# The last recurrent head: two halves of a gate product, and splits and a fetch that come later

## The chip, the cores and the metric

The kernel runs on one core of a Trainium2 chip. The metric is the device time of one execution in microseconds (us), the median of several runs. TensorE is called PE here, VectorE DVE, ScalarE ACT, GpSimd POOL and SyncE SP, as in the profile.

## What is computed

Two transformer blocks over 1024 tokens of width 1024, in float32. The change lies in the first block, in its HGRN2 mixer (six heads of 128 channels, chunks of 64 tokens) and at the start of the output product that follows it:

```python
h = rms_norm(x, norm_mix_g)
u_pool, q_raw, f_raw, i_raw, g_raw = split(h @ w_in)
log_f = log(lb + (1 - lb) * sigmoid(f_raw)); k = (1 - lb) * sigmoid(-f_raw)
q = silu(q_raw); v = i_raw
# per chunk: b = cumsum(log_f)
scores = einsum(q, k, exp(b_t - b_s))          # causal
o = scores @ v + (q * exp(b)) @ state
state = exp(b_last) * state + (k * exp(b_last - b)).T @ v
o = rms(o) * norm_g * silu(g_raw)
x = x + concat([y_pool, y_hgrn]) @ w_out
```

Here the lower bound lb is zero (one layer), so the decay of a step is sigmoid(f_raw).

## The kernel before

Every product of the model is made three times, high part by high part, low by high and high by low, in matmuls of 128x512. Features lie on the 128 partitions and tokens along the free dimension. A product of one weight tile (128 output features, 1024 inputs) takes eight contraction tiles k; each k takes 6 matmuls (three terms, two halves of 512 tokens).

**The program is written out by hand, engine by engine**, with semaphores: each engine works through its own list in order. For a head of the recurrence, `product` (line 798 is its matmul) makes the four projections f, q, i (the value) and g (the output gate). DVE takes each of them out of PSUM (`take`, line 2056). The causal scores are built in seven levels, from neighbouring tokens up to half chunks. For level l, ACT copies two halves of `kd_t` and `qd_t` into a buffer `e_t` (lines 1526 and 1527), PE multiplies them (`level`, line 925), DVE merges the result into `s_t` (`merge`, line 2170; the diagonal at 2155) and multiplies both tiles by decays to prepare the next level (`move`, three instructions, lines 2145 to 2147). ACT's copy for level l waits for move l-1 and for PE's level l-2. Then PE transposes `zv` and `kd_t` (`turn`, line 837), and the state updates, the outputs and the mean of their squares follow (lines 975, 984 and 986, 992).

**Fillers.** `head(h, meanwhile)` on PE has eight places at which another product is put. The first five heads run in a loop and put the next head's projections there. The last head (its code stands behind the loop, in ACT's and DVE's lists under `last`) has its own gate product at place 0, whole, and then parts of the output product of the block: `begin_out(t, part)` makes the contraction tiles `part` of output tile t. An output tile needs the mixed tiles `mix1`, split into `h_hi` (ACT, line 1509, `mix1_hi`) and `h_lo` (DVE, line 2128, `mix_lo`). `h_hi` and `h_lo` hold the input of the projections until then, so ACT waits in front of the first `mix1_hi` until the gate product is finished (`tile_done`, T_OUT1).

**Weights.** POOL splits every weight tile in two instructions (a cast, line 713, and a subtraction, line 715) in the order of use. The split of output tile 1 waits for the end of the gate product, since it overwrites that product's weights. The split of tile 2 comes behind it in POOL's list, and that of tile 3 behind that; tile 3's waits also for the transpose of `zv` and for `sg_t`, over which it is laid. SP loads a raw tile when the split of the tile two places earlier is done.

**The residual** `x_t` shares its memory with `mix1`. It was stored in DRAM (`x_spill`) and is fetched again by one DMA from ACT's queue (line 1562), once seven mixed tiles are split. DVE needs it at line 2301, when the first output tile is finished.

Of the kernel before, what the change touches and what calls it, by code (L numbers as in the profile page):

```python
# [25 lines left out]
ACT = mybir.ActivationFunctionType  # L26
# [5 lines left out]
KT = D // P  # L32
# [8 lines left out]
HEADS = 6  # L41
# [63 lines left out]
T_HEADS = T_POOL + POOL_W // P  # L105
# [60 lines left out]
def two_blocks(nc, dram, out):  # L166
    ctx = ExitStack()
    with ctx:
# [3 lines left out]
        def at(name, shape, address, dtype=F32):  # L172
            return nc.alloc_sbuf_tensor_at(name, shape, dtype, offset=address)
# [4 lines left out]
        h_hi = at("h_hi", [P, KT, SEQ], A_HI, F32R)  # L178
        h_lo = at("h_lo", [P, KT, SEQ], A_LO, F32R)
# [138 lines left out]
        def banks(b, n=2):  # L318
            return psum[:, b:b + n, :].rearrange("p b t -> p (b t)")
# [76 lines left out]
        zf_ready, zq_ready, zv_ready, zg_ready = (sem(f"z{n}_ready") for n in "fqvg")  # L396
# [4 lines left out]
        g_gate = sem("g_gate")  # L401
# [7 lines left out]
        v_turned = sem("v_turned")  # L409
        v_ready = sem("v_ready")  # L410
# [10 lines left out]
        y_ready = sem("y_ready")  # L421
# [362 lines left out]
        def _(pe):  # L784
            def product(n, slot, first_bank, hi, lo, part=range(KT), split=None, halves=range(2), weights=None):

                w_tile_hi, w_tile_lo = weights or (w_hi[:, slot, :], w_lo[:, slot, :])

                pe.wait_ge(weight_split, n + 1)
                for k in part:
                    if split is not None:
                        pe.wait_ge(*split(k))
                    wh, wl = w_tile_hi[:, k * P:(k + 1) * P], w_tile_lo[:, k * P:(k + 1) * P]
                    for j, (w, a) in enumerate(((wh, hi), (wh, lo), (wl, hi))):
                        for t in halves:
                            last = pe.matmul(psum[:, first_bank + t, :], w, a[:, k, t * HALF:(t + 1) * HALF],  # L798
                                             start=(k == 0 and j == 0), stop=(k == KT - 1 and j == 2))
                if part[-1] == KT - 1 and halves[-1] == 1:  # L800
                    last.then_inc(tile_done, 1)
                return last
# [98 lines left out]
                pe.wait_ge(zf_ready, h + 1)  # L901
                product(h * 4 + (T_HEADS + 2), 0, 0, h_hi, h_lo, part)

            def project_g(h):

                pe.wait_ge(zq_ready, h + 1)
                product(h * 4 + (T_HEADS + 3), 1, 2, h_hi, h_lo)

            first_half, second_half = range(KT // 2), range(KT // 2, KT)

# [113 lines left out]
            for j in range(2):  # L1024
                pe.wait_ge(pool_p_ready, j + 1)
                for t in range(2):
                    last = pe.matmul(psum[:, 4 + 2 * j + t, :], pool_w[:, j, :],
                                     pool_p[:, j, t * HALF:(t + 1) * HALF], start=True, stop=True)
# [10 lines left out]
            def begin_out(t, part):  # L1039

                pe.wait_ge(*((zv_ready, HEADS), (zg_ready, HEADS), (o_log, HEADS + 1))[t])
                out_tile(t, part)

            def begin_rest():
                begin_out(1, range(5, 7))
                begin_out(2, range(7))

            head(HEADS - 1, [lambda: project_g(HEADS - 1), lambda: begin_out(0, range(0, 4)),
                             lambda: begin_out(0, range(4, 7)), lambda: begin_out(1, [0]), lambda: begin_out(1, [1]),
                             lambda: begin_out(1, [2, 3]), lambda: begin_out(1, [4]), begin_rest])  # L1050
            for t in range(3):
                out_tile(t, [KT - 1])

# [372 lines left out]
        def _(act):  # L1426
# [87 lines left out]
            def head(h, last):  # L1514
                def level(l):


                    if l == 0:
                        act.wait_ge(qd_start, h + 1)
                    else:  # L1520
                        act.wait_ge(level_moved, h * LEVELS + l)
                    if l >= 2:

                        act.wait_ge(level_done, h * (LEVELS + 1) + l)
                    e = level_parts(e_t[:, l % 2, :], l)
                    act.activation(e[:, :, 0, :], level_parts(kd_t[:, :], l)[:, :, 0, :], ACT.Copy)
                    act.activation(e[:, :, 1, :], level_parts(qd_t[:, :], l)[:, :, 1, :], ACT.Copy)\
                       .then_inc(level_ready, 1)

                def begin_mix(*tiles):  # L1530
                    if last:
                        for d in tiles:
                            mix1_hi(d)


                act.wait_ge(zq_ready, h + 1)
                act.activation(q_t[:, :], zq[:, :], ACT.Sigmoid).then_inc(q_gate, 1)
                act.wait_ge(zf_ready, h + 1)
                act.activation(decays[:, 0:SEQ], zf[:, :], ACT.Sigmoid).then_inc(f_ready, 1)
                act.activation(kd_t[:, :], zf[:, :], ACT.Sigmoid, scale=-1.0).then_inc(kd_start, 1)  # L1540
                act.activation(k_t[:, :], zf[:, :], ACT.Sigmoid, scale=-1.0).then_inc(k_ready, 1)
                act.wait_ge(kd_start, h + 1)
                level(0)
                level(1)

                act.wait_ge(y_ready, h + 1)
                act.wait_ge(zg_ready, h + 1)
                act.activation(sg_t[:, :], zg[:, :], ACT.Sigmoid).then_inc(g_gate, 1)
                if last:

                    act.wait_ge(tile_done, T_OUT1)
                begin_mix(0, 1)
                level(2)
                begin_mix(2, 3, 4, 5, 6)
                level(3)

                act.wait_ge(v_turned, h + 1)
                act.activation(v_tok[:, :, :].rearrange("p c v -> p (c v)"), banks(6), ACT.Copy).then_inc(v_ready, 1)
                if last:

                    act.wait_ge(mix_split, KT - 1)
                    act.dma_start(x_t[:, 0:KT - 1, :].rearrange("p d t -> p (d t)"),
                                  x_spill[:, 0:(KT - 1) * SEQ]).then_inc(x_back, 16)
                level(4)
                level(5)
                level(6)

                act.wait_ge(kd_turned, h + 1)
                act.activation(kd_tok[:, :, :].rearrange("p c k -> p (c k)"), banks(6), ACT.Copy)\
                   .then_inc(kd_tok_ready, 1)  # L1570

                act.wait_ge(o_done, h + 1)
                act.activation(e_t[:, 1, :], banks(6), ACT.Square).then_inc(o_sq, 1)
                act.wait_ge(o_mean, h + 1)
                act.activation(e_t[:, 0, :], banks(4), ACT.Ln, scale=1.0 / P, bias=eps1[:, :]).then_inc(o_log, 1)
                act.wait_ge(o_log, h + 2)
                act.activation(e_t[:, 0, :], e_t[:, 0, :], ACT.Exp, scale=-0.5).then_inc(o_inv, 1)
# [423 lines left out]
        def _(dve):  # L2001
# [56 lines left out]
            def take_f(h):  # L2058
                take(zf, h * 4 + T_HEADS, 6 if isinstance(h, int) and h == 0 else 0, zf_ready)
# [7 lines left out]
            def take_g(h):  # L2067
                take(zg, h * 4 + (T_HEADS + 3), 2, zg_ready)
# [62 lines left out]
            def head(h, last):  # L2131
# [5 lines left out]
                def move(l):  # L2137


                    n, s = SEQ >> (l + 1), 1 << l  # L2140
                    decay, twice = decay_of(l), 2 * SEQ - (2 * SEQ >> (l + 1))
                    q, k = level_parts(qd_t[:, :], l)[:, :, 1, :], level_parts(kd_t[:, :], l)[:, :, 0, :]

                    dve.wait_ge(level_ready, h * LEVELS + (l + 1))
                    dve.tensor_tensor(q, q, decay[:, :, 0:1].to_broadcast([P, n, s]), ALU.mult)
                    dve.tensor_tensor(k, k, decay[:, :, 1:2].to_broadcast([P, n, s]), ALU.mult)
                    dve.tensor_tensor(decays[:, twice:twice + n], decay[:, :, 0], decay[:, :, 1], ALU.mult)\
                       .then_inc(level_moved, 1)
# [24 lines left out]
                def begin_mix(*tiles):  # L2173
                    if last:
                        for d in tiles:
                            mix_lo(0, d, mix1)
# [6 lines left out]
                dve.tensor_tensor(qd_t[:, :], q_t[:, :], decays[:, 0:SEQ], ALU.mult).then_inc(qd_start, 1)  # L2183
                move(0)
                move(1)
                take_g(h)
                merge_diagonal()
                merge(0, 4)
                begin_mix(0)
                move(2)  # L2190
                begin_mix(1)
                merge(1, 5)
                begin_mix(2, 3)

                dve.wait_ge(g_gate, h + 1)
                dve.tensor_tensor(sg_t[:, :], zg[:, :], sg_t[:, :], ALU.mult).then_inc(sg_ready, 1)
                move(3)
                begin_mix(4, 5, 6)
                if not last:

                    dve.wait_ge(k_ready, h + 1)
                    take_f(h + 1)
                merge(2, 4)
                move(4)
                merge(3, 5)
                move(5)
                merge(4, 6)
# [597 lines left out]
```

## Time and profile before

| | us |
|---|---|
| median of 3 runs | 2596.09 (2593.04 to 2596.7) |
| the profiled execution | 2595.25 |
| its span, first to last instruction | 2593.5 |
| PE busy | 2545.7 (98% of the span) |
| DVE busy | 1514.2 (58%) |
| POOL busy | 947.8 (37%) |
| ACT busy | 676.4 (26%) |

The last head runs from about 381 us to 439 us of the span, under 3% of it. A busy time over the whole kernel says little about such a short stretch. There the timelines of the single engines are to be read side by side: where PE is idle and who released it, and what the releasing engine did before.

### The profile page before, as it was taken

The page shows a single profiled execution, that of the slowest core. Times are in us where ns is not written, and L with a number is a line of the kernel's source. Part 1 is how long each engine was busy: PE and PEld are TensorE (multiplying, and loading weights), DVE is VectorE, ACT ScalarE, POOL GpSimd, SP SyncE. Part 2 cuts the span into 40 slices and gives each one's busy share as a digit, 9 for nine tenths or more (in the row PEclk, how much of TensorE's full clock was granted, in tenths as well). Part 3 has the DMA queues.
Part 4 walks back from the last instruction along what each step waited for, and adds up shares of the span by engine and source line. Part 5 has one row for each costly group of instructions (what it writes and reads, how often), then busy time and mean ns, then how long its engine had stood idle before and what let it go on. Part 6 is the DMA issues. An engine that isn't in the chain of part 4 may idle for free.

```text
span 2593.5 us, 37645 instructions
## 1 busy us (share of the span) xinstructions
PE 2545.7 (98%) x14373; PEld 2081.0 (80%) x14373; DVE 1514.2 (58%) x1617; ACT 676.4 (26%) x921; POOL 947.8 (37%) x558
## 2 busy tenths in 40 slices
PE   8999998999999999999999999999999999999997
PEld 7788886878888888887777788888888888888886
DVE  6755566843335666667777786354455555555555
ACT  4233443443332000013333313201211111111114
POOL 2222222387874333333222232333333333333334
PEclk9999998999999999999999999999999999999999
DMA  6111112333434222223111111113111111111111
GB/s 208 39 41 32 32 40 90 124 98 121 129 108 170 97 97 97 97 73 123 33 39 38 39 41 49 49 49 114 45 45 48 49 49 49 49 49 49 49 49 74
DMA packets 212830, 186.04 MB, mean 72 GB/s; under 512 B 15343, under 2 KB 184986, under 8 KB 211738
## 3 DMA queue, kind: packets, MB, share of 16 engines
q1 hardware_dynamic: 189604, 122.92, 15.6%
q10 hardware_dynamic: 23158, 62.18, 6.6%
q8 instruction: 46, 0.75, 0.1%
q14 instruction: 22, 0.18, 0.0%
HBM read 151.51 MB, written 35.33 MB: 72 GB/s over the span
## 4 chain that ended last, share of the span: by engine, by line
PE 86%; DVE 9%; ACT 2%; issue 2%; DMA 1%; DVEq 0%; ACTq 0%; SPq 0%
PE psum L798 48%; PE psum L817 16%; PE psum L1089 11%; PE psum L1299 3%; PE psum L837 1%; PE psum L925 1%; DVE ffn_gate L2693 1%; DVE x_t L2326 1%; PE psum L1228 1%; DVE h_lo L2025 1%; PE psum L1413 1%; PE psum L1209 1%; DVE sq_sum L2020 1%; DVE ffn_val L2697 0%; DVE ffn_gate L2697 0%
## 5 line engine op out<-in xcount | busy, mean ns | idle before, releaser
L713 POOL CAST w_hi<-w_raw 128x1024 fp32r<-128x1024 f32 x180 | 204.8, 1138 | 1489.4 <-issue 763.9
L798 PE MATMUL psum<-h_hi,w_hi 128*128 128x512 f32 x1744 | 551.8, 397 | 9.1 <-DVE h_lo L2128 6.5
L798 PE MATMUL psum<-h_lo,w_hi 128*128 128x512 f32 x1744 | 539.6, 391 | 0.0
L798 PE MATMUL psum<-h_hi,w_lo 128*128 128x512 f32 x1744 | 538.9, 390 | 0.0
L715 POOL TENSOR_TENSOR w_lo<-w_raw,w_hi 128x1024 fp32r<-128x1024 f32 x180 | 478.2, 2657 | 14.4
L798 PEld LDWEIGHTS psum<-h_hi,w_hi 128*128 128x128 f32 x1744 | 322.1, 188 | 83.6 <-issue 18.9
L798 PEld LDWEIGHTS psum<-h_hi,w_lo 128*128 128x128 f32 x1744 | 328.2, 188 | 69.6
L798 PEld LDWEIGHTS psum<-h_lo,w_hi 128*128 128x128 f32 x1744 | 328.1, 188 | 69.5
L2326 DVE TENSOR_TENSOR x_t<-x_t,psum 128x512 f32<-128x512 f32 x416 | 281.1, 684 | 171.2 <-PE psum L817 162.9
L2685 DVE TENSOR_TENSOR ffn_z<-psum,rinv 128x1024 f32<-128x1024 f32 x44 | 53.9, 1225 | 273.9 <-PE psum L798 266.0
L817 PE MATMUL psum<-down_hi,w_hi 128*128 128x512 f32 x512 | 199.6, 390 | 2.2 <-DVE x_t L2326 2.0
L817 PE MATMUL psum<-down_hi,w_lo 128*128 128x512 f32 x512 | 199.2, 389 | 0.0
L817 PE MATMUL psum<-down_lo,w_hi 128*128 128x512 f32 x512 | 199.2, 389 | 0.0
L2497 DVE SCALAR_TENSOR_TENSOR conv_t<-u_t,cols,conv_t 128x1024 f32<-128x1024 f32 x120 | 179.6, 1496 | 2.4
L817 PE MATMUL psum<-ffn_hi,w_hi 128*128 128x512 f32 x320 | 127.0, 397 | 4.0 <-DVE x_t L2326 3.4
L817 PE MATMUL psum<-ffn_lo,w_hi 128*128 128x512 f32 x320 | 124.7, 390 | 0.0
L817 PE MATMUL psum<-ffn_hi,w_lo 128*128 128x512 f32 x320 | 124.7, 390 | 0.0
L817 PEld LDWEIGHTS psum<-down_hi,w_hi 128*128 128x128 f32 x512 | 96.1, 188 | 23.7 <-DVE x_t L2326 3.9
L817 PEld LDWEIGHTS psum<-down_hi,w_lo 128*128 128x128 f32 x512 | 96.1, 188 | 20.1
L817 PEld LDWEIGHTS psum<-down_lo,w_hi 128*128 128x128 f32 x512 | 96.1, 188 | 19.6
L1745 ACT ACTIVATE down_hi<-down_in 128x1024 fp32r<-128x1024 f32 x32 | 32.1, 1052 | 280.3 <-DMA down_in<-act_rows 280.3
L753 POOL TENSOR_TENSOR mlp_s_lo<-mlp_s_sum,mlp_s_hi 128x512 fp32r<-128x512 f32 x60 | 78.1, 1335 | 19.9 <-ACT mlp_s_hi L1633 19.9
(374 smaller groups left out, 3910.5 us busy)
## 6 DMA issues: line engine op xcount, KB each, us to landing
w_raw<-in_w_in SPq DMA_DIRECT2D x124, 256.0 KB, 3.1
w_raw<-in_w_up SPq DMA_DIRECT2D x120, 256.0 KB, 3.2
w_raw<-in_w_down SPq DMA_DIRECT2D x108, 256.0 KB, 2.7
act_rows<-mlp_a ACTq DMA_DIRECT2D x32, 512.0 KB, 3.6
down_in<-act_rows ACTq DMA_DIRECT2D x32, 512.0 KB, 3.6
w_raw<-in_w_out SPq DMA_DIRECT2D x32, 256.0 KB, 3.1
mlp_raw<-in_w_up SPq DMA_DIRECT2D x32, 256.0 KB, 3.7
x_in<-in_x SPq DMA_DIRECT2D x8, 512.0 KB, 8.1
```

Of the source, the lines that this page charges most:

```text
L713: pool.tensor_copy(hi, w_raw[:, slot, :]).then_inc(weight_hi, 1)
L715: pool.tensor_tensor(lo, w_raw[:, slot, :], hi.bitcast(F32), ALU.subtract).then_inc(weight_split, 1)
L753: done = pool.tensor_tensor(lo[:, :], full[c], hi[:, :].bitcast(F32), ALU.subtract)
L798: last = pe.matmul(psum[:, first_bank + t, :], w, a[:, k, t * HALF:(t + 1) * HALF], start=(k == 0 and j == 0), stop=(k == KT - 1 and j == 2))
L817: last = pe.matmul(psum[:, 4 + g % 4, :], w, a[k][:, t * HALF:(t + 1) * HALF], start=(k == 0 and j == 0), stop=(k == 1 and j == 2))
L837: last = pe.transpose(psum[:, dst_bank + c // 4, (c % 4) * P:(c % 4 + 1) * P], block_in, ident[:, :])
L1089: last = pe.matmul(psum[:, bank, :], w, a[:, :], start=start and kk == part[0] and j == 0, stop=stop and kk == part[-1] and j == 2, skip_g ...
L1299: last = pe.matmul(psum[:, bank + t, :], w, a[:, t * HALF:(t + 1) * HALF], start=(k == 0 and j == 0), stop=(k == 3 and j == 2))
L1745: act.activation(down_hi[b][j][:, :], down_in[b][j][:, :], ACT.Copy).then_inc(act_hi_ready, 1)
L2326: dve.tensor_tensor(x_d, x_d, psum[:, 4 + g % 4, :], ALU.add).then_inc(down_added, 1)
L2497: dve.scalar_tensor_tensor(acc, u_t[:, c % 2, tap:tap + SEQ], w, acc, ALU.mult, ALU.add)\
L2685: dve.tensor_tensor(ffn_z[:, part, :], banks(2 * part), rinv[:, :], ALU.mult).then_inc(ffn_read, 1)
```

## The change

On PE the last head's gate product is cut in two. Its first four contraction tiles stay in place 0, and the other four go to place 1, behind levels 0 and 1. The parts of the output product move one place back and are grouped otherwise. On ACT the order of the last head becomes levels 0 to 3, the value's copy, the gate's sigmoid, the high parts of mixed tiles 0 to 3, level 4, the high parts of 4 to 6, level 5, the fetch of the residual, level 6. On DVE the gate is taken behind merge 1 instead of behind move 1, and the low parts follow the gate's multiplication. In the loop's five heads nothing changes but the place of one conditional that does not apply to them.

```diff
-            def project_g(h):
+            def project_g(h, part=range(KT)):
                 pe.wait_ge(zq_ready, h + 1)
-                product(h * 4 + (T_HEADS + 3), 1, 2, h_hi, h_lo)
+                product(h * 4 + (T_HEADS + 3), 1, 2, h_hi, h_lo, part)
...
-            head(HEADS - 1, [lambda: project_g(HEADS - 1), lambda: begin_out(0, range(0, 4)),
-                             lambda: begin_out(0, range(4, 7)), lambda: begin_out(1, [0]), lambda: begin_out(1, [1]),
-                             lambda: begin_out(1, [2, 3]), lambda: begin_out(1, [4]), begin_rest])
+            head(HEADS - 1, [lambda: project_g(HEADS - 1, first_half), lambda: project_g(HEADS - 1, second_half),
+                             lambda: begin_out(0, range(0, 4)), lambda: begin_out(0, range(4, 7)),
+                             lambda: begin_out(1, [0]), lambda: begin_out(1, [1, 2]), lambda: begin_out(1, [3, 4]),
+                             begin_rest])
...
                 level(0)
                 level(1)
-
-                act.wait_ge(y_ready, h + 1)
-                act.wait_ge(zg_ready, h + 1)
-                act.activation(sg_t[:, :], zg[:, :], ACT.Sigmoid).then_inc(g_gate, 1)
+                if not last:
+                    gate()
+                level(2)
+                level(3)
+                take_v()
                 if last:
-
+                    gate()
                     act.wait_ge(tile_done, T_OUT1)
-                begin_mix(0, 1)
-                level(2)
-                begin_mix(2, 3, 4, 5, 6)
-                level(3)
-
-                act.wait_ge(v_turned, h + 1)
-                act.activation(v_tok[:, :, :].rearrange("p c v -> p (c v)"), banks(6), ACT.Copy).then_inc(v_ready, 1)
+                begin_mix(0, 1, 2, 3)
+                level(4)
+                begin_mix(4, 5, 6)
+                level(5)
                 if last:
 
                     act.wait_ge(mix_split, KT - 1)
                     act.dma_start(x_t[:, 0:KT - 1, :].rearrange("p d t -> p (d t)"),
                                   x_spill[:, 0:(KT - 1) * SEQ]).then_inc(x_back, 16)
-                level(4)
-                level(5)
                 level(6)
...
                 move(0)
                 move(1)
-                take_g(h)
+                if not last:
+                    take_g(h)
                 merge_diagonal()
                 merge(0, 4)
-                begin_mix(0)
                 move(2)
-                begin_mix(1)
                 merge(1, 5)
-                begin_mix(2, 3)
+                if last:
+                    take_g(h)
+                    move(3)
 
                 dve.wait_ge(g_gate, h + 1)
                 dve.tensor_tensor(sg_t[:, :], zg[:, :], sg_t[:, :], ALU.mult).then_inc(sg_ready, 1)
-                move(3)
-                begin_mix(4, 5, 6)
+                begin_mix(0, 1)
                 if not last:
+                    move(3)
 
                     dve.wait_ge(k_ready, h + 1)
                     take_f(h + 1)
+                begin_mix(2)
                 merge(2, 4)
+                begin_mix(3)
                 move(4)
+                begin_mix(4, 5, 6)
                 merge(3, 5)
```

`gate` and `take_v` are the two pieces of ACT's list that were written in line before.

## Rows read from the trace of the kernel before

**Rows 1.** The page, part 4: shares of the chain that ended last.
```profile
PE 86%; DVE 9%; ACT 2%; issue 2%; DMA 1%; DVEq 0%; ACTq 0%; SPq 0%
```

**Rows 2.** Chain in order of time, 355 to 470 us: start, us, what.
```profile
439.31 27.24 PE psum L798 x120
```

**Rows 3.** PE's timeline, 345 to 470 us: start, us, instruction, count [idle before <-releaser].
```profile
391.71 0.76 PE L942 MATMUL psum<-q_t,k_t 128*32 128x32 f32 x64
395.70 0.31 PE L925 MATMUL psum<-e_t 128*32 128x16 f32 x12 [2.20 <-issue]
402.52 1.19 PE L798 MATMUL psum<-h_hi,w_hi 128*128 128x512 f32 x2 [6.51 <-DVE h_lo L2128]
...
408.11 0.83 PE L798 MATMUL psum<-h_hi,w_hi 128*128 128x512 f32 x2
411.09 1.04 PE L837 MATMUL psum<-ident,zv 128*128 128x128 f32 x8
...
425.78 1.09 PE L837 MATMUL psum<-ident,kd_t 128*128 128x128 f32 x8
```

**Rows 4.** DVE's timeline of the same stretch.
```profile
389.51 0.69 DVE L2145 TENSOR_TENSOR qd_t<-qd_t,decays 128x512 f32<-128x512 f32 x1 [1.34 <-ACT e_t L1527]
...
392.75 0.77 DVE L2145 TENSOR_TENSOR qd_t<-qd_t,decays 128x512 f32<-128x512 f32 x1 [1.34 <-ACT e_t L1527]
393.45 2.82 DVE L2146 TENSOR_TENSOR kd_t<-kd_t,decays 128x512 f32<-128x512 f32 x1
396.19 1.25 DVE L2147 TENSOR_TENSOR decays<-decays 128x256 f32<-128x256 f32 x1
397.37 1.21 DVE L2056 TENSOR_TENSOR zg<-psum,rinv 128x1024 f32<-128x1024 f32 x1
398.50 1.33 DVE L2155 COPY_PREDICATED s_t<-pair_mask,psum 128x1024 f32<-128x1024 uint32 x1
400.02 1.30 DVE L2170 COPY_PREDICATED s_t<-pair_mask,psum 128x512 f32<-128x512 uint32 x1 [0.18 <-DVE s_t L2155]
...
411.12 3.50 DVE L2128 TENSOR_TENSOR h_lo<-mix,h_hi 128x1024 fp32r<-128x1024 f32 x3
414.52 0.72 DVE L2170 COPY_PREDICATED s_t<-pair_mask,psum 128x512 f32<-128x512 uint32 x1
416.27 2.27 DVE L2145 TENSOR_TENSOR qd_t<-qd_t,decays 128x512 f32<-128x512 f32 x1 [1.03 <-ACT e_t L1527]
```

**Rows 5.** POOL's timeline, 330 to 500 us.
```profile
391.94 1.04 POOL L713 CAST w_hi<-w_raw 128x1024 fp32r<-128x1024 f32 x1 [7.35 <-issue]
393.06 2.66 POOL L715 TENSOR_TENSOR w_lo<-w_raw,w_hi 128x1024 fp32r<-128x1024 f32 x1
395.67 1.50 POOL L713 CAST w_out_hi<-w_raw 128x1024 fp32r<-128x1024 f32 x1
397.25 2.42 POOL L715 TENSOR_TENSOR w_out_lo<-w_raw,w_out_hi 128x1024 fp32r<-128x1024 f32 x1
412.29 3.22 POOL L713 CAST w_out_hi<-w_raw 128x1024 fp32r<-128x1024 f32 x1 [12.63 <-PE psum L837]
415.59 2.40 POOL L715 TENSOR_TENSOR w_out_lo<-w_raw,w_out_hi 128x1024 fp32r<-128x1024 f32 x1
```

**Rows 6.** ACT's timeline, 345 to 470 us.
```profile
387.20 1.05 ACT L1541 ACTIVATE k_t<-zf 128x1024 f32<-128x1024 f32 x1
...
392.02 0.70 ACT L1527 ACTIVATE e_t<-qd_t 128x512 f32<-128x512 f32 x1
398.68 1.06 ACT L1548 ACTIVATE sg_t<-zg 128x1024 f32<-128x1024 f32 x1 [5.96 <-DVE zg L2056]
```

**Rows 7.** Busy time by stretch; PEclk is the granted TensorE clock (1.00 is 2.4 GHz).
```profile
396.00:402.00 6.00, 0.01 (x1) 0.00 (x0) 5.82 (x6) 3.33 (x4) 3.58 (x2) 0.69 0.46 138
406.00:408.00 2.00, 2.00 (x6) 1.61 (x5) 2.00 (x3) 2.00 (x4) 0.00 (x0) 0.50 0.00 0
```

**Rows 8.** DMA issues by line, 355 to 480 us: queue, count, KB each, us to landing.
```profile
x_t<-x_spill ACTq DMA_DIRECT2D x1, 3584.0 KB, 12.6
```

More of the change, by code:

```diff
@@ L1542, in head, with gate, take_v @@
                 act.wait_ge(kd_start, h + 1)
+                def gate():
+                    act.wait_ge(y_ready, h + 1)
+                    act.wait_ge(zg_ready, h + 1)
+                    act.activation(sg_t[:, :], zg[:, :], ACT.Sigmoid).then_inc(g_gate, 1)
+                def take_v():
+                    act.wait_ge(v_turned, h + 1)
+                    act.activation(v_tok[:, :, :].rearrange("p c v -> p (c v)"), banks(6), ACT.Copy).then_inc(v_ready, 1)
                 level(0)
                 level(1)
-                act.wait_ge(y_ready, h + 1)
-                act.wait_ge(zg_ready, h + 1)
-                act.activation(sg_t[:, :], zg[:, :], ACT.Sigmoid).then_inc(g_gate, 1)
+                if not last:
[3 more added lines that the diff above has]
+                take_v()
                 if last:
+                    gate()
                     act.wait_ge(tile_done, T_OUT1)
-                begin_mix(0, 1)
-                level(2)
-                begin_mix(2, 3, 4, 5, 6)
-                level(3)
-                act.wait_ge(v_turned, h + 1)
-                act.activation(v_tok[:, :, :].rearrange("p c v -> p (c v)"), banks(6), ACT.Copy).then_inc(v_ready, 1)
+                begin_mix(0, 1, 2, 3)
+                level(4)
+                begin_mix(4, 5, 6)
+                level(5)
                 if last:
```

## The prediction

> **What bounds the kernel now.** I read the shares of the chain that ended last first: PE holds 86% of it and DVE 9% [rows 1]. Behind the last head PE runs without a gap, 120 matmuls in 27.24 us, or 0.227 us each, so six matmuls (one contraction tile k) cost 1.36 us [rows 2]. The time of the kernel therefore moves by as much as the point moves at which that last block starts: 439.31 us. Everything after it is the same program with the same distances.
>
> So the question is what sets 439.31. PE's timeline comes next. PE finishes the gate product at 391.71, makes the diagonal and levels 0 and 1, stops for 2.20 us in level 1 with no releaser shown, and then is idle for 6.51 us until DVE has split the first mixed tile [rows 3]. That idle time is what the change can fill. But PE is not what is late there. DVE's timeline shows a queue that hardly pauses from 392.75 until its last moves: its waits in the rows are fractions of a microsecond up to about 1 us, while single instructions take four times their usual time [rows 4]. POOL's timeline, laid beside it, shows why. The multiplication of `kd_t` at 393.45 takes 2.82 us where one of this shape takes 0.69, and it ends just after POOL's subtraction (393.06 to 395.72). The `decays` product at 396.19 waits out POOL's cast (395.67 to 397.17), and the one at 416.27 takes 2.27 us beside POOL's subtraction (415.59 to 417.99). Instructions that read PSUM, as the gate's take at 397.37 and the merge at 398.50, keep their 1.2 to 1.3 us beside POOL's subtraction of 397.25 to 399.67 [rows 4, 5]. **DVE instructions with both inputs in SBUF and POOL's splits exclude each other; those with an input in PSUM do not.** In this stretch DVE loses (2.82 - 0.69) + (1.25 - 0.4) + (2.27 - 0.69) = 4.6 us to it. The 0.4 is my estimate for 256 columns, between the 0.69 of 512 and a fixed part.
>
> **The change, part by part.**
>
> *The gate product in halves.* Its start on PE is 391.71 - 48 x 0.227 = 380.8 [rows 2, 3]; the first 24 matmuls end at 386.3. The diagonal needs `k_t`, which ACT ends at 388.25 [rows 6], and level 1 needs ACT's copy that ends at 392.72 [rows 6]. So PE now idles about 2 us ahead of the diagonal and again ahead of level 1, ends level 1 at about 393.4, and starts the second half there. At the full rate that half takes 5.45 us and ends at 398.9.
>
> The clock adds to that. In the kernel before the granted clock averages 0.69 over 396 to 402 and is 0.50 in 406 to 408 (1.2 GHz): it fell after PE had given up full-size matmuls at 391.7 and done only small ones and nothing [rows 3, 7]. The new order gives up full-size matmuls for 393.4 - 386.3 = 7.1 us, and before they were missing for 10.8 us. I take it that the clock falls here too, as this is the nearest row. The 12 matmuls from 402.52 to 408.11 then took 5.59 us instead of 2.72, so a fall costs 2.9 us [rows 3]; not falling costs 0. I take 2.9 and get **T = 401.7 for the end of the gate product** (398.9 if the clock stays).
>
> The 2.20 us stop in level 1 has no releaser and 180 small matmuls in front of it [rows 3]. It cost nothing before, since PE was waiting for DVE afterwards. In the new order it would lie before T. I take 0, since PE now idles twice ahead of that place and whatever is fetched has time to arrive, with 2.2 as the other end. The Trainium skill (Runtime: NRT & Kernel Launch, Instruction fetch mechanics) says that the instruction buffer is refilled in blocks while the engine runs and that crossing a block is mostly hidden; by it the term is 0 too, and the row before shows a stop that is not hidden, if it is that.
>
> *DVE until T.* Move 1 is no longer beside POOL's splits, because these wait for the gate product's end. It ends at 392.75 + 0.6 + 0.6 + 0.3 = 394.3 instead of 397.4. Diagonal and merge 0 (1.15 each), move 2 (0.6 + 0.6 + 0.2) and merge 1 (1.15) follow: 399.2. ACT makes the copies for levels 2 and 3 meanwhile. DVE then waits for T: **a new wait of 2.5 us**, and behind it are queued the take, moves 3 to 6, merges 2 to 6 and all seven splits.
>
> *DVE after T.* Durations from start to start are 0.1 less than in the rows. Take 1.13, move 3 1.3, gate multiplication 1.14, splits 0 to 2 3.4: 7.0 us in all. ACT does not hold it up: transpose (1.0, rows 3), value copy 1.0 and sigmoid 1.0 are done at T + 3.1, and one high part per 0.96 follows.
>
> POOL, however, starts the split of output tile 1 at T, that of tile 2 right behind and that of tile 3 behind that: three casts of 1.04 and three subtractions of 2.4, 10.3 us [rows 5]. Before, these lay at 391.9 to 399.7 and at 412.3 to 418, and 4.6 us of them hurt. Now all stand beside the take (1.1 us hidden) and the pile of SBUF instructions behind it. If the two take turns, as at 393.45 and 396.19, the seven DVE microseconds become 7.0 + 9.3 = 16.3: split 2 ends at T + 0.1 + 16.3 = 418.1. The rest has POOL out of its way: merge 2 0.65, split 3 1.14, move 4 1.3, splits 4 to 6 3.4, merge 3 0.65, move 5 1.27: 426.5. ACT's copy for level 6 takes 1.15 to 427.7, move 6 1.25 to 428.9. The transpose of `kd_t` on PE then ends at 428.9 + 0.15 + 0.9 = **429.9, against 426.9 before** (425.78 + 1.09, rows 3).
>
> The contention has a lower end. At 411.12 DVE made three splits in 3.50 us, one after the other, while POOL's cast, ready at 412.29, took 3.22 instead of 1.04 [rows 4, 5]: there POOL waited for a whole streak. If it does so again behind the gate's multiplication, part of its work moves beside merges and waits and some 2 us are saved. If there were no contention at all, 9.3 would be. I take turns, since two of the three collisions went that way, and keep 2 us below for the range.
>
> The Trainium skill (SBUF — State Buffer, SBUF: two separate sides) says that such a DVE instruction and a GpSimd one take a shared pair of ports whole, first come first served. It agrees with 2.82 us at 393.45, and speaks against this change. It says nothing of who is next when both wait, which is where the 2 us lie.
>
> *PE after the transpose.* Before, from 426.87 to 439.31, 12.44 us, with four k tiles as fillers. The new list has tile k 0 of output tile 1, then 1 and 2, then 3 and 4 there: five. The one more costs 1.36, as nothing else is late: 13.7 us, 429.9 + 13.7 = 443.6. All other fillers fit into the time in which PE waits for DVE: the mixed tiles arrive every 1.14 us or slower and cost 1.36.
>
> *The residual's fetch.* Its 3.5 MB take 12.6 us [rows 8]. The last split that it waits for ends at about 424.6, so it lands at 437.2, and the first addition comes over 14 us after 443.6: nothing. ACT's level 6 stands behind that wait in its queue, but needs move 5, which DVE makes after those splits anyway. Output tiles 2 and 3 are needed after 443.6, and POOL is done by about 418: nothing.
>
> **Sum.** 443.6 - 439.31 = +4.3 us. Split by cause: 2.5 for the wait for T, 9.3 - 4.6 = 4.7 for more contention, 1.4 for the k tile, and 4.3 less for DVE's old pauses, which the new waits swallow. On the profiled execution that is 2599.5; the median of the runs lies 0.84 above it, so 2600.4. As most bounds lie below, I say 2600.
>
> **Rivals.**
> 1. *The clock does not fall* in the seven microseconds. T is 398.9, the sum +4.3 - 2.8 = +1.5: 2597.6. For it: two of the gaps are short, with matmuls between. Against it: the fall in the rows after a like pause.
> 2. *POOL stays out of the way* (its instructions wait for DVE's streaks, as at 412.29). Then PE's 6.5 us idle stretch is really filled. Without contention the sum is +4.3 - 9.3 = -5.0, with the clock staying too -7.8: 2591.1 and 2588.3. Against it are 393.45, 396.19 and 416.27.
> 3. *The slower side: PE's stop without a releaser moves into the gate product.* It delays T by 2.2 and all behind it: +6.5, 2602.6. It decides as soon as over 0.9 us of the stop are left before T. For it: the stop came 228 matmuls into this code, and the second half now stands at just that count (24 + 64 + 128 = 216 ahead of it). Against it: PE idles over 4 us ahead of it.
> 4. *Nothing of this is on the path.* I rule it out, since 439.31 hangs on DVE.
>
> **How the numbers follow.** The forecast gets 0.45, and spans 0 to +5.5 with its bounds. Rival 1 gets 0.15, rival 2 0.17, rival 3 0.23. About 0.2%, 5.2 us, is what a measurement can tell from no change. Faster by more: most of rival 2, 0.13. Slower by more: nearly all of rival 3 and the upper edge of the forecast, 0.27. The rest, 0.60, is within. The range reaches from rival 2's upper case, 2591, to rival 3 with a little more contention, 2604.
>
> **What would show each step.** PE: 24 matmuls, a gap ahead of L942, a gap ahead of level 1, then 24 matmuls up to about 401.7, at 0.45 us each for part of them. Granted clock 0.50 somewhere in 392 to 400. DVE: `kd_t` of move 1 at 0.69 instead of 2.82, a wait of some 2.5 us ahead of the take, and 2 to 3 us in the `qd_t` or `kd_t` of move 3 and in one of the splits. POOL: six instructions without pause from T on. PE: first matmul of the output product at about 412, transpose of `kd_t` at 429, the block of 120 matmuls at 443.6. The forecast is wrong if POOL's instructions are stretched instead of DVE's, or if T lies under 399.

## The result

The changed kernel takes 2599.64 us in the median of 20 runs (2596.77 to 2603.79), the kernel before 2596.34 (2593.04 to 2601.89). The ratio is 1.0014 with a 95% interval of 1.0008 to 1.0021: slower by 3.3 us in the medians, 2 to 5.5 us by the interval. That is a difference: the interval does not reach 1. The prediction had named 0.2%, 5.2 us, as what a measurement can tell; 20 runs of each tell less than that. 2600 was forecast, in the range 2591 to 2604.

The profiled execution of the changed kernel took 2603.79 us with a span of 2602.0, 8.5 more than the span of before. Only part of that is the change's: this execution is the slowest of the 20, 4.15 us above their median, and the profiled execution of before (2595.25) lies 1.09 us below the median of that kernel. To read the last head by itself I use a distance **D: from the end of ACT's `k_t` sigmoid to the start of the block of 120 matmuls** (the end of the four matmuls in front of it). In the kernel before it is 439.31 - 388.25 = 51.06 us [rows 2, 6]. In the changed kernel it is 443.64 - 388.75 = 54.89. **The change costs 3.83 us there.** Of the other 4.7 us, 0.5 arose ahead of it and 4.2 behind the block's start, and in both stretches the two programs are the same.

PE's timeline of the changed kernel (start, us, instruction, count, idle before and its releaser), and the last row of the chain in order of time:

```profile
388.85 0.86 PE L942 MATMUL psum<-q_t,k_t 128*32 128x32 f32 x64 [2.00 <-ACT k_t L1542]
393.23 1.05 PE L925 MATMUL psum<-e_t 128*32 128x16 f32 x64 [2.01 <-ACT e_t L1528]
394.21 1.22 PE L798 MATMUL psum<-h_hi,w_hi 128*128 128x512 f32 x2
398.65 1.04 PE L798 MATMUL psum<-h_hi,w_lo 128*128 128x512 f32 x2
399.50 0.65 PE L798 MATMUL psum<-h_hi,w_hi 128*128 128x512 f32 x2
402.26 1.04 PE L837 MATMUL psum<-ident,zv 128*128 128x128 f32 x8
412.61 1.19 PE L798 MATMUL psum<-h_hi,w_hi 128*128 128x512 f32 x2 [8.04 <-DVE h_lo L2134]
428.73 1.09 PE L837 MATMUL psum<-ident,kd_t 128*128 128x128 f32 x8 [0.16 <-DVE decays L2153]
441.76 1.88 PE L992 MATMUL psum<-e_t,ones 128*128 128x512 f32 x4
```
```profile
443.64 27.27 PE psum L798 x120
```

The two gaps of 2.0 us ahead of the diagonal and of level 1 are there. The second half of the gate product runs from 394.2 to 402.3, its first 12 matmuls at half rate. The idle stretch that the change was to fill is longer than before: 8.04 us instead of 6.51 [rows 3]. Its releaser is again DVE's first split.

DVE's timeline of the changed kernel shows why (line 2152 answers 2146 of before, 2134 answers 2128):

```profile
393.82 0.69 DVE L2152 TENSOR_TENSOR kd_t<-kd_t,decays 128x512 f32<-128x512 f32 x1
398.82 1.32 DVE L2176 COPY_PREDICATED s_t<-pair_mask,psum 128x512 f32<-128x512 uint32 x1
402.46 1.22 DVE L2062 TENSOR_TENSOR zg<-psum,rinv 128x1024 f32<-128x1024 f32 x1 [2.33 <-PE psum L798]
404.20 2.85 DVE L2152 TENSOR_TENSOR kd_t<-kd_t,decays 128x512 f32<-128x512 f32 x1
406.98 1.05 DVE L2153 TENSOR_TENSOR decays<-decays 128x64 f32<-128x64 f32 x1
407.95 1.21 DVE L2203 TENSOR_TENSOR sg_t<-zg,sg_t 128x1024 f32<-128x1024 f32 x1
409.09 8.66 DVE L2134 TENSOR_TENSOR h_lo<-mix,h_hi 128x1024 fp32r<-128x1024 f32 x3
```

and POOL's timeline of the changed kernel:

```profile
402.59 1.04 POOL L713 CAST w_hi<-w_raw 128x1024 fp32r<-128x1024 f32 x1 [17.49 <-issue]
403.70 2.80 POOL L715 TENSOR_TENSOR w_lo<-w_raw,w_hi 128x1024 fp32r<-128x1024 f32 x1
406.46 1.49 POOL L713 CAST w_out_hi<-w_raw 128x1024 fp32r<-128x1024 f32 x1
408.03 3.35 POOL L715 TENSOR_TENSOR w_out_lo<-w_raw,w_out_hi 128x1024 fp32r<-128x1024 f32 x1
411.33 2.03 POOL L713 CAST w_out_hi<-w_raw 128x1024 fp32r<-128x1024 f32 x1
413.44 3.23 POOL L715 TENSOR_TENSOR w_out_lo<-w_raw,w_out_hi 128x1024 fp32r<-128x1024 f32 x1
```

Move 1 is free of POOL (0.69 instead of 2.82 us, rows 4). In exchange all six of POOL's instructions stand without a pause from the end of the gate product on, and three splits of DVE take 8.66 us, where three took 3.50 [rows 4]. In this stretch both engines wait for each other.

### The profile page after: what moved, and what is told of

The parts are those of the page before. It is cut to its first block, busy times and chain, and to the rows that moved or that the text cites. A ratio compares the mean times of both kernels' runs of the same rounds, so it can differ in the third digit from the quotient of the medians.

```text
span 2602.0 us, 37645 instructions
## 1 busy us (share of the span) xinstructions
PE 2554.4 (98%) x14373; PEld 2088.8 (80%) x14373; DVE 1519.8 (58%) x1617; ACT 676.0 (26%) x921; POOL 946.9 (36%) x558
## 4 chain that ended last, share of the span: by engine, by line
PE 85%; DVE 9%; ACT 2%; issue 2%; DMA 1%; DVEq 0%; ACTq 0%; SPq 0%
PE psum L798 47%; PE psum L817 16%; PE psum L1090 11%; PE psum L1300 3%; PE psum L837 1%; PE psum L925 1%; DVE ffn_gate L2703 1%; DVE x_t L2336 1%; PE psum L1229 1%; DVE h_lo L2031 1%; PE psum L1414 1%; DMA x_t<-x_spill 1%; PE psum L1210 1%; DVE sq_sum L2026 1%; DVE ffn_val L2707 0%
```

## The experiments

Each kernel was run ten times (e7 four times). It has a time against the kernel before on the same chip, and D from its profiled execution. D is the finer measure, since it leaves out what varies elsewhere. It comes from one execution each, but a like distance shows how much such a number varies: from one head's `k_t` sigmoid to the next one's, in the last four intervals ahead of the last head, where all twelve programs are the same, the twelve traces have 58.78 to 58.95 us. Differences in D of over 0.2 us are therefore read as the kernel's.

D has three parts. "Last move" is the time from the end of the `k_t` sigmoid to the end of DVE's last move (move 6). "PE late" is what passes from there to the start of the transpose of `kd_t` on PE; 0.05 or 0.06 means that PE was waiting. The rest, from that start to the block, is 13.5 us in all kernels with four contraction tiles there (before, e1, e4, e8, e10) and 14.9 in all with five.

| kernel | D, us | last move | PE late | ratio to before (95%) |
|---|---|---|---|---|
| before | 51.06 | 36.18 | 1.35 | |
| changed | 54.89 | 39.92 | 0.06 | 1.0014 (1.0008 to 1.0021) |
| e1 before, three splits cut to 4 columns | 45.09 | 31.51 | 0.06 | 0.9979 (0.9970 to 0.9989) |
| e2 changed, the same cut | 47.77 | 31.59 | 1.28 | 0.9984 (0.9975 to 0.9994) |
| e3 changed, PE kept busy in its gaps | 52.32 | 37.37 | 0.05 | 1.0006 (0.9997 to 1.0016) |
| e4 before, splits deferred | 45.13 | 31.54 | 0.05 | 0.9977 (0.9967 to 0.9986) |
| e5 changed, splits deferred | 46.76 | 31.82 | 0.05 | 0.9986 (0.9976 to 0.9995) |
| e6 changed, gate product whole | 49.74 | 34.79 | 0.05 | 1.0001 (0.9992 to 1.0011) |
| e7 before, PE's list of the changed one | 62.33 | 42.62 | 4.82 | 1.0051 (1.0035 to 1.0066) |
| e8 before, deferred, residual's fetch late | 43.99 | 30.39 | 0.05 | 0.9979 (0.9969 to 0.9988) |
| e9 changed, whole, deferred | 46.30 | 30.33 | 1.10 | 0.9981 (0.9972 to 0.9991) |
| e10 as e9, a filler ahead of level 6 | 46.33 | 30.32 | 2.48 | 0.9980 (0.9971 to 0.9990) |

### e1 and e2: POOL's three splits taken away

POOL works on 4 of the 1024 columns of output tiles 1, 2 and 3, so both kernels leave out most of these splits and compute three output tiles with wrong weights; all waits stay. Shown is the edit in short:

```diff
+                some = slice(0, 4 if isinstance(n, int) and T_OUT1 < n < T_OUT1 + 4 else 1024)
-                pool.tensor_copy(hi, w_raw[:, slot, :]).then_inc(weight_hi, 1)
+                pool.tensor_copy(hi[:, some], w_raw[:, slot, some]).then_inc(weight_hi, 1)
...
-                        weights=None if t < 2 else w_out_parts[t - 2])
+                        weights=None)
```

> The kernel before, but POOL's splits of output tiles 1, 2 and 3 work on 4 of 1024 columns only (their waits stay), and PE takes whatever lies in the two ordinary weight slots for tiles 2 and 3; so three of the block's output tiles are computed with wrong weights. D is the distance from the end of ACT's k_t sigmoid to the block of 120 matmuls: 51.1 us in the kernel before, 54.9 in the changed one. Contention theory (DVE's queue with two SBUF inputs and POOL's splits exclude each other, and DVE is the bound): the 4.6 us that DVE loses come back, and 2 more where the pauses close up, D about 44.5 and 6 to 7 us faster than before. Rival (PE's idle stretch is bound by the order of the list, not by DVE): D falls by under 2 us.

> The changed kernel with the same three splits cut to 4 columns. Contention theory: 9.3 us of blocking go, of which 1 to 2 turn into waits for ACT: D about 47.2, 7.5 to 8.5 us less than the changed kernel's 54.9 and 3 to 4 us faster than the kernel before, but still 2 to 3 us behind e1, since T, the end of the gate product, stays near 402 and one more contraction tile stands behind the transpose. Rival (the difference between the two kernels is contention alone): e2 equals e1 within 1 us. Rival (the halves are to blame, not contention): e2 stays within 2 us of the changed kernel.

Measured: D falls by 5.97 us on the kernel before and by 7.12 on the changed one. The medians agree: 2590.37 and 2592.69 against 2596.38. In e1, 4.67 us of the gain are DVE's, which is the 4.6 that the prediction counted as lost to POOL, and 1.29 are PE's lateness of before, which goes too. DVE's timeline of e2 has no long instruction left:

```profile
400.13 1.23 DVE L2063 TENSOR_TENSOR zg<-psum,rinv 128x1024 f32<-128x1024 f32 x1 [1.75 <-PE psum L799]
401.87 0.69 DVE L2153 TENSOR_TENSOR kd_t<-kd_t,decays 128x512 f32<-128x512 f32 x1
404.15 3.49 DVE L2135 TENSOR_TENSOR h_lo<-mix,h_hi 128x1024 fp32r<-128x1024 f32 x3
```

So the two engines exclude each other, and in both kernels it is DVE's queue that the contention lengthens. Both rivals of e2 fall as they were stated for D: without the splits the changed kernel is still 2.68 us behind, and it did not stay near 54.9. But DVE's last move ends at the same time in both (31.51 and 31.59), so for DVE's queue by itself the first rival holds. The 2.68 are the one contraction tile more behind the transpose (1.36) and PE, which in e2 is late by 1.28. PE runs there at half rate for a while, which it does not in e5, the same order with the splits deferred. Busy time from 408 to 410 us (length, then busy time and instructions of PE, PEld, DVE, ACT and POOL, the granted clock, DMA share, GB/s), of e2 and then of e5; the granted clock is 0.50 (1.2 GHz) and 1.00:

```profile
408.00:410.00 2.00, 2.00 (x6) 1.61 (x5) 2.00 (x4) 2.00 (x3) 0.00 (x0) 0.50 0.81 243
```
```profile
408.00:410.00 2.00, 2.00 (x11) 1.65 (x10) 2.00 (x4) 2.00 (x3) 0.00 (x0) 1.00 0.00 0
```

Why it fell in the one and not in the other is not shown; PE had been idle for 3.29 us ahead of it in both.

### e3: the clock

The edit, in short: 8 matmuls of 128x512 ahead of the diagonal and 10 ahead of level 1, their results unused.

```diff
+            def keep_busy(count):
+                pe.wait_ge(zv_ready, HEADS)
+                for j in range(count):
+                    pe.matmul(psum[:, j % 2, :], w_hi[:, 1, 0:P], h_hi[:, 0, 0:HALF], start=True, stop=True)
...
                 meanwhile[0]()
+                if isinstance(h, int):
+                    keep_busy(8)
...
                 level(0, 4)
+                if isinstance(h, int):
+                    keep_busy(10)
                 level(1, 5)
```

> The changed kernel with idle-time matmuls added in the last head: 8 of 128x512 ahead of the diagonal and 10 ahead of level 1, into two free PSUM banks, results unused. Theory (the granted clock fell over the 7 us without full-size matmuls, and T is on the path): the clock stays at 1.00, the 24 matmuls of the second half take 5.5 us instead of 8.1, T comes 2.7 to 2.9 us earlier and D goes from 54.9 to about 52.0; against the kernel before about +1. Rival (DVE's pile behind T absorbs it, the clock costs nothing): T earlier, D within 0.7 us of 54.9.

Measured: D 52.32, 2.57 less. Busy time by stretch, in the same columns, of the changed kernel and then of e3:

```profile
390.00:394.00 4.00, 1.83 (x121) 1.75 (x125) 2.69 (x5) 1.22 (x3) 0.00 (x0) 0.50 0.02 4
394.00:398.00 4.00, 4.00 (x32) 3.20 (x24) 3.82 (x5) 1.15 (x2) 0.00 (x0) 0.50 0.01 4
```
```profile
390.00:394.00 4.00, 3.85 (x139) 3.13 (x139) 2.69 (x5) 1.21 (x3) 0.00 (x0) 1.00 0.01 4
394.00:398.00 4.00, 4.00 (x23) 3.31 (x19) 3.82 (x5) 1.17 (x2) 0.00 (x0) 1.00 0.00 0
```

With matmuls in the gaps the granted clock stays at 1.00 (2.4 GHz) where it was 0.50 (1.2 GHz), the transpose of `zv` starts at 399.58 instead of 402.26, and the gain reaches D almost whole. It is not a gain in contention: move 3 and the three splits lose 8.1 us to POOL here and 8.2 in the changed kernel. The clock is a term of the path, 2.6 us.

### e4 and e5: the splits moved, with all work done

The split of tile 1 goes to the memory of tile 2 and waits for move 1; the split of tile 2 goes to the gate's weight slot and waits, like that of tile 3 behind it, for the last move. The edit, in short:

```diff
-                elif isinstance(n, int) and n in (T_OUT1 + 2, T_OUT1 + 3):
...
+                elif isinstance(n, int) and n == T_OUT1 + 1:
+                    for read in (k_ready, q_ready):
+                        pool.wait_ge(read, HEADS)
+                    pool.wait_ge(level_moved, (HEADS - 1) * LEVELS + 2)
+                    hi, lo = w_out_parts[0]
+                elif isinstance(n, int) and n == T_OUT1 + 2:
+                    pool.wait_ge(tile_done, T_OUT1)
+                    pool.wait_ge(level_moved, HEADS * LEVELS)
+                    hi, lo = w_hi[:, 1, :], w_lo[:, 1, :]
```

> The kernel before with POOL's splits moved out of DVE's way: tile 1 goes to the memory of tile 2 and is split once move 1 is made, tile 2 goes to the gate's slot and is split, like tile 3, once the last move is made. Same result as the reference. Contention theory: almost all of e1's gain with all work done: D 44.5 to 45.5, 5.5 to 7 us faster than before, and no DVE instruction of the last head over 1.4 us. Rival (the late splits hold up output tile 2 or 3, or POOL's later tiles): D falls but PE waits for a weight within the block of 120, and the gain is under 3 us.

> The changed kernel with POOL's splits moved as in the run on the kernel before: tile 1 after move 1, tiles 2 and 3 after the last move. Same result as the reference. Contention theory: all of what the cut splits gave, D about 47.8 (cut splits 47.8, changed kernel 54.9), 3 to 4 us faster than the kernel before, and behind the kernel before with the same deferral (D 45.1) by 2.6. Rival (after the deferral both orders are alike, since PE's idle stretch is filled): D within 0.7 us of 45.1.

Measured: 45.13 and 46.76. In e4, POOL's first two instructions stand beside DVE's PSUM readers and the rest behind its last move:

```profile
393.31 1.04 POOL L724 CAST w_out_hi<-w_raw 128x1024 fp32r<-128x1024 f32 x1 [10.09 <-DVE decays L2158]
394.43 2.38 POOL L726 TENSOR_TENSOR w_out_lo<-w_raw,w_out_hi 128x1024 fp32r<-128x1024 f32 x1
418.70 1.04 POOL L724 CAST w_hi<-w_raw 128x1024 fp32r<-128x1024 f32 x1 [21.89 <-DVE decays L2158]
```

Deferring gives all that cutting gave: 5.93 us on the kernel before (cut: 5.97) and 8.13 on the changed one (cut: 7.12, and 8.33 at DVE's last move, since PE was late in e2). **e4 beats both kernels**, with all work done: 2590.20 us against 2596.38 of the kernel before. e5 stays 1.63 behind it, of which 1.36 is the contraction tile behind the transpose. 2.6 was expected, after the 2.68 of e2, and most of the difference is PE's lateness there.

Some contention is left in e5 (and in e9). POOL's first subtraction meets move 2, and DVE makes up for it in its wait for the gate product:

```profile
395.20 1.77 DVE L2162 TENSOR_TENSOR qd_t<-qd_t,decays 128x512 f32<-128x512 f32 x1
399.94 1.23 DVE L2073 TENSOR_TENSOR zg<-psum,rinv 128x1024 f32<-128x1024 f32 x1 [0.91 <-PE psum L809]
```

### e6 and e7: all but the halves, and PE's list alone

e6 makes the gate product whole in place 0 and leaves place 1 empty; e7 gives the kernel before PE's new list and nothing else. The edit of e6, in short:

```diff
-            head(HEADS - 1, [lambda: project_g(HEADS - 1, first_half), lambda: project_g(HEADS - 1, second_half),
+            head(HEADS - 1, [lambda: project_g(HEADS - 1), lambda: None,
```

> The changed kernel with the gate product whole in place 0 again; ACT's, DVE's and the other parts of PE's order stay changed. If the halves cost what the walk says, T is 391.7 again and DVE's wait ahead of the take goes: D falls from 54.9 to about 50 to 51, level with the kernel before (51.1) or up to 1 us below it. Rival (the later mixed tiles are what costs, not the halves): D stays above 53.5.

> The kernel before with PE's list of the changed one (the gate product in halves, the fillers one place back) and ACT's and DVE's lists as before. DVE takes the gate behind move 1 and waits there for T, with the merges, moves and splits queued behind. Theory: T about 402, DVE stands from 394.3 to T, D near 61 to 62, about 10 us slower than the kernel before. Rival (PE-bound stretch): D within 3 us of the changed kernel's 54.9.

Measured: e6 49.74, e7 62.33. The halves cost 54.89 - 49.74 = 5.15 us in the changed kernel; everything else in the change together (ACT's and DVE's lists, the later fetch, the fillers one place back) gains 51.06 - 49.74 = 1.3. That is DVE's last move 1.39 earlier and PE no longer late (1.30), less 1.36 for the contraction tile behind the transpose. In e7, DVE's timeline shows the wait at the place that the change moved it from:

```profile
399.68 1.23 DVE L2057 TENSOR_TENSOR zg<-psum,rinv 128x1024 f32<-128x1024 f32 x1 [7.13 <-PE psum L798]
```

### e8: the residual's fetch

e8 is e4 with ACT's wait and DMA of `x_t` behind level 5, as in the change.

> The kernel before with the deferred splits and, from the change, only the residual's fetch behind level 5 in ACT's list. In the run with deferred splits ACT stands at that fetch until the seventh mixed tile is split, and DVE then waits 1.03 us for level 4's copy. Theory: that wait goes, D falls from 45.1 to about 44.2, 7 us faster than the kernel before; the fetch lands at about 427 + 1, and nothing waits for it. Rival (another engine ends last in that stretch): D stays at 45.1 within 0.3.

Measured: D 43.99, 1.14 less than e4. DVE's timelines of e4 and then of e8 differ in the first multiplication of move 4:

```profile
411.86 0.69 DVE L2156 TENSOR_TENSOR qd_t<-qd_t,decays 128x512 f32<-128x512 f32 x1 [1.03 <-ACT e_t L1538]
```
```profile
410.39 0.67 DVE L2156 TENSOR_TENSOR qd_t<-qd_t,decays 128x512 f32<-128x512 f32 x1
```

The wait of 1.03 us is gone. The time of whole runs does not show it (0.9979 against 0.9977): 1 us is below what these intervals tell, so this gain rests on one trace of each.

### e9 and e10: whole product and deferred splits together, and a filler moved

> The changed kernel with the gate product whole in place 0 and with the deferred splits; ACT's and DVE's changed order stays. If the halves' cost (5.1 us with contention) and the contention add up, D is 49.7 - 6 to 46.8 - 2, so 43.7 to 44.8, with one contraction tile more behind the transpose than the kernel before has. Rival (without contention the halves cost nothing, since DVE's wait for T was 0.9 us in the deferred version): D stays at 46.8 within 0.7.

> As the run before, but contraction tile 0 of output tile 1 stands ahead of level 6 again, and tiles 1, then 2 and 3, then 4 behind the transpose as in the kernel before. Theory (each contraction tile behind the transpose costs its 1.36 us): the distance from the transpose to the block of 120 falls from 14.9 to 13.5 us; D falls by 1.36 less what the tile delays level 6, so 0.5 to 1.4 us below the run before, 43 to 44. Rival (the fillers fit into waits of PE there): D unchanged within 0.3.

e10 differs from e9 in PE's list: tile 0 of output tile 1 ahead of level 6, one fewer behind the transpose. Measured: 46.30 and 46.33. **Both rivals hold**, and e9's expectation of 43.7 to 44.8 is missed. In e10 the transpose of `kd_t` comes 1.4 us later than in e9, and the tail is 1.4 shorter:

```profile
421.23 1.09 PE L848 MATMUL psum<-ident,kd_t 128*128 128x128 f32 x8
```
```profile
419.85 1.09 PE L848 MATMUL psum<-ident,kd_t 128*128 128x128 f32 x8
```

(e10 first, then e9; both have `k_t` at 388.4.) With POOL out of the way PE works without a pause from 405.7 us to the transpose in both, and is late by 1.10 and 2.48 us, so a filler only changes its side. With the splits deferred DVE's last move ends at the same time with the new order of ACT's and DVE's lists (e9, 30.33) as with the old one (e8, 30.39).

## Why the prediction was right, point by point

**What bounds.** DVE's queue behind 392.75 is what the block's start hangs on. e1, e2, e4 and e5 show it: work taken off POOL, which nothing in that stretch waits for, moves the block by 6 to 8 us. But "PE is not what is late there" holds only for the idle stretch. At the end of the head PE is the late one in the kernel before: DVE's last move ends at 424.43, and the transpose of `kd_t` starts at 425.78 [rows 3], 1.35 us later, behind a stretch with the clock at 1.2 GHz for most of the time. In the changed kernel it starts 0.06 after the last move. The last instruction of move 6 before and changed, and busy time by stretch of before (granted clock 0.55 and 0.60):

```profile
424.27 0.16 DVE L2147 TENSOR_TENSOR decays<-decays 128x8 f32<-128x8 f32 x1
```
```profile
428.51 0.16 DVE L2153 TENSOR_TENSOR decays<-decays 128x8 f32<-128x8 f32 x1
```
```profile
422.00:424.00 2.00, 2.00 (x6) 1.14 (x4) 1.43 (x3) 1.02 (x2) 0.00 (x0) 0.55 0.95 409
424.00:426.00 2.00, 2.00 (x35) 1.87 (x35) 1.06 (x3) 0.00 (x0) 0.00 (x0) 0.60 0.88 308
```

**T, the end of the gate product.** Forecast 401.7, which is 13.45 us after `k_t`; the trace has 402.26, 13.5 after it. The gaps are 2.00 and 2.01 us, the loss to the clock 2.7 at the end of the gate product (402.26 against 399.58 in e3) for 2.9 forecast.

**The stop without a releaser** (rival 3) does not come in the changed kernel. It comes in all profiled kernels with the whole product in front (before, e1, e4, e6, e8, e9 and e10), for 1.92 to 2.48 us, each time 116 small matmuls into levels 0 and 1; and it doesn't in e2, e3, e5 or e7. PE's timeline of e6:

```profile
394.08 0.30 PE L925 MATMUL psum<-e_t 128*32 128x16 f32 x12 [2.21 <-issue]
```

Taking 0 was right. What it is stays open; e3 has no gaps to speak of ahead of that place and no stop either, so that the idle time of PE is what averts it is not shown.

**DVE's new wait** ahead of the take: 2.33 for 2.5.

**Contention.** Blocked time in the changed kernel, against the same instructions in e2: (2.85 - 0.69) + (1.05 - 0.22) + (8.66 - 3.49) = 8.2 us; 9.3 was forecast and 2 less named as the lower end. They did take turns. The 1.1 us less is spread over the five turns: DVE lost 2.16 us where POOL's subtraction takes 2.4 by itself, 0.83 where its cast takes 1.04, and 5.17 where the three of them take 5.84, so each turn cost DVE some 0.2 us less than the forecast counted. Why is not shown.

**Behind the transpose:** 443.64 - 428.73 = 14.91 against 439.31 - 425.78 = 13.53 [rows 2, 3], 1.38 more for 1.36 forecast. So D rises by 3.83 for 4.3. **The two came this near in part by luck.** The forecast put the transpose itself at 0.9 us where the row has 1.09, and 12.44 + 1.36 is 13.8 and not 13.7; added up rightly its walk gives some 4.6. The contention that was 1.1 us too dear made up for that.

**The split of the sum by cause was the weak step.** It gave the contention 4.7 us of the difference, the wait 2.5 and the tile 1.4, less 4.3 for DVE's pauses that vanish, as if they added. Of those 4.3 about 1.3 were never DVE's, but PE's lateness of before, which vanishes. And the terms don't add. The four runs that cross whole or halves with splits as before or deferred say it (D, and in brackets the end of DVE's last move after `k_t`):

| | splits as before | splits deferred |
|---|---|---|
| whole product | 49.74 (34.79) | 46.30 (30.33) |
| in halves | 54.89 (39.92) | 46.76 (31.82) |

The halves cost 5.15 us with contention and 0.46 without; the contention costs 3.44 with the whole product and 8.13 with the halves. In D the interaction looks larger than it is, since e9 is the one of the four in which PE ends last, by 1.10 us. At DVE's last move the halves cost 5.13 with contention and 1.49 without. So 3.6 of their 5.1 us are **one mechanism, not a second term**: the end of the gate product gates POOL's queue of three splits, and moving that end back drops all of them on DVE's densest stretch. The other 1.5 are mostly waits of DVE for the gate product and for ACT's sigmoid (0.91 and 0.32 us in e5, none in e9). The step that failed in e9's expectation was the same one, adding what had been measured beside the other, together with leaving PE out. The sum against before came out because each instruction was walked in its place, contention and all.

**Rival 1** (the clock stays) fell with the 0.50 above; e3 shows what it would have been, +1.3 us in D, for +1.5 worked out. **Rival 2** (POOL stays out of the way) fell too, but its price was roughly sound: -5.0 us against the kernel before was worked out for no contention, and e5 has 46.76 - 51.06 = -4.3.

**The later fetch** costs nothing, as forecast: it took 11.1 us instead of 12.6 and DVE's first addition waits for PE. On its own it gains 1.1 us (e8), which the prediction did not see, since ACT's wait for the seventh split was not followed to level 4's copy.

**What is not the change's.** The medians differ by 3.3 us where D differs by 3.83; the interval of the ratio holds both. The 4.2 us that the profiled execution lost behind the start of the block arose where nothing was changed, and they go with its being the slowest of 20; which instructions they lie in was not followed up.

## What to carry to other kernels

When an instruction is moved, list what its completion releases on other queues. Here the gate product's end released three weight splits on POOL, and their new place cost more than the gap on PE that was to be filled. An idle stretch of the busiest engine is worth filling only once it is known which engine's queue ends it; here the cheaper step was to move the work of an engine with plenty of slack (POOL, 37% busy) beside instructions that it does not exclude, 6 us for a few waits. When DVE was freed, PE came to end last in some of the kernels, so each distance should be read for both engines. And costs that share a mechanism should be measured crossed, not one by one.

## What the runs showed of the hardware

Who goes first when DVE and POOL both want to work on SBUF is not settled by these runs. In the changed kernel they took strict turns over three splits (8.66 us). In e6 a cast of POOL, released while DVE was in the same three splits, waited for all of them:

```profile
404.54 3.48 DVE L2134 TENSOR_TENSOR h_lo<-mix,h_hi 128x1024 fp32r<-128x1024 f32 x3
```
```profile
404.88 4.04 POOL L713 CAST w_out_hi<-w_raw 128x1024 fp32r<-128x1024 f32 x1 [6.84 <-DVE sg_t L2203]
```

as it had in the kernel before [rows 4, 5]. Two more casts lost in this way. The one of 4 columns in e1 (0.19 us elsewhere) took 2.55, to the end of the three splits, and the one in e7 waited through the three products of move 3 and three splits:

```profile
407.56 2.55 POOL L714 CAST w_out_hi<-w_raw 128x4 fp32r<-128x4 f32 x1 [16.18 <-PE psum L838]
```
```profile
414.84 5.39 POOL L713 CAST w_out_hi<-w_raw 128x1024 fp32r<-128x1024 f32 x1 [7.26 <-DVE sg_t L2197]
```

In all four cases the cast came fresh from a semaphore while DVE was busy. But that does not decide it: in e3 such a cast, released by the same multiplication as in e6 and e7, waited for one split only, and so did a cast of 4 columns in e2 (0.73 us):

```profile
409.06 1.77 POOL L713 CAST w_out_hi<-w_raw 128x1024 fp32r<-128x1024 f32 x1 [1.48 <-DVE sg_t L2213]
```

A sum should keep both ends.
